# Last expert pair of a mixture-of-experts encoder layer: weights loaded in pieces, the waiting sums moved, the final norm shared among three engines

## What is computed

```python
def block_ffn(args):                  # one expert e and the tokens routed to it
    e, tok, wt = args
    xb = x_pad[tok]
    hid = jax.nn.silu(xb @ w1[e]) * (xb @ w3[e])     # 1024 -> 512, twice
    return (hid @ w2[e]) * wt[:, None]               # 512 -> 1024
...
x = x + g2 * moe_ffn(h, ...)
return rms_norm(x) * final_g          # x * rsqrt(mean(x*x) + eps) * final_g
```

## Time and profile before

| | |
|---|---|
| median of three runs | 721.17 us |
| the profiled execution | 720.32 us |
| its span, first to last instruction | 718.5 us |
| PE busy | 671.7 us (93%) |
| DVE, ACT, POOL busy | 346.4, 174.1, 56.0 us |
| read from memory | 252.84 MB |

### The profile page before, as it was taken

The page is one execution under the profiler, slowest core; times in us unless marked ns, Lnnn a source line. Parts: engine busy times, 40 slices in busy tenths (PEclk is TensorE's granted clock), DMA queues, the critical chain, the costliest instruction groups (busy, mean ns, idle before and its releaser), DMA issues.

```text
span 718.5 us, 9181 instructions
## 1 busy us (share of the span) xinstructions
PE 671.7 (93%) x3685; PEld 364.2 (51%) x3685; DVE 346.4 (48%) x648; ACT 174.1 (24%) x309; POOL 56.0 (8%) x55
## 2 busy tenths in 40 slices
PE   2799999999998799999999999898999999989893
PEld 2477787866878433443443443453434344334341
DVE  3554988798977713333333343333233443332236
ACT  4433468323324210210210210111021111110104
POOL 2016900100000100000000000000000000000000
PEclk9999999999999899999999999999999999999997
DMA  9998355665359699999999999999999999999952
GB/s 333 388 376 299 118 176 204 237 234 234 117 235 352 255 399 421 425 426 429 424 428 425 428 425 427 412 425 428 425 425 430 426 424 429 423 425 429 426 239 117
DMA packets 39147, 253.19 MB, mean 352 GB/s; under 512 B 4160, under 2 KB 4544, under 8 KB 26304
## 3 DMA queue, kind: packets, MB, share of 16 engines
q1 hardware_dynamic: 34560, 243.82, 83.1%
q0 software_dynamic: 2624, 4.74, 1.8%
q10 hardware_dynamic: 1920, 4.04, 1.5%
HBM read 252.84 MB, written 4.19 MB: 358 GB/s over the span
## 4 chain that ended last, share of the span: by engine, by line
PE 71%; DMA 21%; DVE 4%; SPq 1%; issue 1%; ACT 1%; POOLq 0%; DVEq 0%
PE bank L963 24%; PE bank L654 18%; DMA ring<-in_w 17%; PE bank L972 12%; DMA ring<-in_w_mod 3%; PE bank L980 3%; PE bank L981 2%; PE bank L926 2%; SPq L483 1%; PE bank L778 1%; DVE x L1825 1%; PE bank L1002 1%; DMA xg_rows<-x_rows,keep 1%; PE bank L934 1%; PE bank L606 1%
## 5 line engine op out<-in xcount | busy, mean ns | idle before, releaser
L963 PE MATMUL bank<-ring,low 128*64 128x512 f32 x944 | 228.2, 599 | 11.7 <-DMA ring<-in_w 11.0
L963 PEld LDWEIGHTS bank<-ring,low 128*64 128x64 f32 x944 | 75.0, 138 | 132.1 <-issue 131.0
L1825 DVE TENSOR_TENSOR x<-x,bank 128x512 f32<-128x512 f32 x136 | 84.4, 682 | 79.5 <-PE bank L981 79.5
L972 PE MATMUL bank<-ring,low 128*64 128x512 f32 x432 | 114.0, 596 | 1.0 <-DVE x L1825 0.9
L972 PEld LDWEIGHTS bank<-ring,low 128*64 128x64 f32 x432 | 35.0, 137 | 65.2 <-issue 63.5
L1815 DVE SCALAR_TENSOR_TENSOR y_raw<-bank,keep,g2b 128x512 f32<-128x512 f32 x32 | 24.0, 751 | 87.4 <-PE bank L972 87.4
L1936 DVE TENSOR_TENSOR low<-low,bank 128x512 f32<-128x512 f32 x16 | 11.0, 688 | 102.5 <-PE bank L963 102.5
L980 PE MATMUL bank<-y_hi,slot_tok 128*128 128x512 f32 x128 | 53.5, 418 | 0.2 <-DVE y_lo L1820 0.2
L981 PE MATMUL bank<-y_lo,slot_tok 128*128 128x512 f32 x128 | 50.3, 393 | 0.0
L1444 ACT COPY low<-bank 128x512 f32<-128x512 f32 x16 | 9.4, 586 | 165.0 <-PE bank L934 165.0
L1454 ACT CAST y_hi<-y_raw 128x512 fp32r<-128x512 f32 x32 | 19.8, 618 | 108.2 <-DVE y_raw L1815 108.2
(11 more groups left out here) (274 smaller groups left out, 880.6 us busy)
## 6 DMA issues: line engine op xcount, KB each, us to landing
ring<-in_w SPq DMA_DIRECT2D x82, 2048.0 KB, 26.6
ring<-in_w_mod SPq DMA_DIRECT2D x11, 2048.0 KB, 11.9
mid<-in_w SPq DMA_DIRECT2D x10, 2048.0 KB, 28.1
ring<-in_w_in SPq DMA_DIRECT2D x4, 2048.0 KB, 22.9
ring<-in_w SPq DMA_DIRECT2D x8, 1024.0 KB, 8.6
ring<-in_w_out SPq DMA_DIRECT2D x2, 2048.0 KB, 10.3
x<-in_x SPq DMA_DIRECT2D x4, 512.0 KB, 5.3
mid<-in_w_mod SPq DMA_DIRECT2D x1, 2048.0 KB, 23.8
```

Of the source, the lines that this page charges most:

```text
L963: last = mm(bk[e * CAP:(e + 1) * CAP, :], xb[:, k, e * CAP:(e + 1) * CAP], unit(n % SLOTS, KD)[:, k, :], start=k == 0, stop=k == KD - 1)
L972: last = mm(bk[e * CAP:(e + 1) * CAP, :], hid_t[:, k, e * CAP:(e + 1) * CAP], unit(n % SLOTS, KF)[:, k, hf * 512:(hf + 1) * 512], start=k ...
L1825: return v.tensor_tensor(acc[:, t, c], acc[:, t, c], bk[:, :], ALU.add)
```

## The change

- SP loads the last pair's units in pieces (`last_pair_units`). w1 and w3 come as two halves over k, the first halves of both experts ahead of the second halves. w2 comes as the left 512 columns, and the right 512 columns in two halves over k. A transfer for the first piece of the second expert now stands ahead of the second piece of the first. PE waits for the first pieces, and inside the products for the others.
- In the last pair the waiting sums use eight different banks and wait for no add. Of the second four, three are made after up product B and the fourth after `turn_hid`. The down product waits for four adds in place of eight.
- ACT loads the root's table after the last pair's hidden copy. DVE adds the first of the final sums between `weighted` and `low_part` of the second half.
- In the final norm ACT squares half rows: four left halves, one instruction that makes the root's bias of their sums, then for each tile the right half and the root. DVE scales the right halves alone. For the left halves GpSimd multiplies by final_g and ACT scales the product. A store waits for both.

```diff
+            def last_pair_units(k):
+                w, kk = ((w1_r, KD), (w3_r, KD), (w2_r, KF))[k // 2]
+                pieces = (((slice(0, kk // 2), slice(0, 512)), (slice(kk // 2, kk), slice(0, 512))) if k < 4 else
+                          ((slice(0, kk), slice(0, 512)), (slice(0, kk // 2), slice(512, D)),
+                           (slice(kk // 2, kk), slice(512, D))))
+                for i, (r, c) in enumerate(pieces):
+                    for e in range(2):
+                        n = FIRST[LAST] + k + e
+                        if i == 0:
+                            slot_used_up(n - SLOTS)
+                        src = w[:, bass.ds(experts_of(LAST)[e], 1), r, c].rearrange("p e k n -> p (e k) n")
+                        done = landed[n % SLOTS] if i == len(pieces) - 1 else (begun[k + e], middle_in[e])[i]
+                        sp.dma_start(unit(n % SLOTS, kk)[:, r, c], src).then_inc(done, 16)
...
-            for n in range(SLOTS + 4, UNITS):
+            for n in range(SLOTS + 4, FIRST[LAST]):
...
+            for k in range(0, UPP, 2):
+                last_pair_units(k)
...
             for t in range(NT):
                 sp.wait_ge(fin, t + 1)
+                sp.wait_ge(fin_low, t + 1)
...
+            def sum_bank(p, g):
+                return ((TB, CA, Y0, Y1, G0, G1, A1, A3) if p == LAST else SUM_BANKS + SUM_BANKS)[g]
...
+                        if k == KD // 2 and n0 == FIRST[LAST]:
+                            pe.wait_ge(landed[n % SLOTS], landed_at(n))
...
+                        if n0 == FIRST[LAST] and hf == 1:
+                            if k == 0:
+                                pe.wait_ge(middle_in[e], 16)
+                            elif k == KF // 2:
+                                pe.wait_ge(landed[n % SLOTS], landed_at(n))
...
-                    if g >= 4:
+                    if g >= 4 and p < LAST:
...
-                if before:
+                if p == LAST:
+                    pe.wait_ge(sil_ready, p + 1)
+                    combine_before(p, range(4, 7))
+                    summed(1)
+                elif before:
                     combine_before(p, range(4, 8))
-                summed(5)
+                    summed(5)
                 pe.wait_ge(hid_ready, p + 1)
                 turn_hid().then_inc(t_done, 1)
+                if p == LAST:
+                    combine_before(p, range(7, 8))
...
-                summed(8)
+                summed(4 if p == LAST else 8)
...
                 nc.scalar.copy(hid_t.rearrange("p k s -> p (k s)"), TB[:, :]).then_inc(hidt_ready, 1)
+                if to_come == 0:
+                    a(rstd[:, 0:1], col["eps"], ACT.Sqrt).then_inc(fin_table, 1)
...
+            def halfs_square(t, hf, sums):
+                act.wait_ge(acc_done, 8 * LAST + HALVES_FIRST.index(2 * t + hf) + 1)
...
+                a(unread, acc[:, t, c], ACT.Square, accum_out=sums[:, t:t + 1]).then_inc(fin_ssq, 1)
+
+            def low_half_scaled(t):
+                act.wait_ge(fin_rec, t + 1)
+                act.wait_ge(fin_gain, t + 1)
+                a(acc[:, t, 0:512], gained[:, t, :], ACT.Copy, scale=rstd[:, t:t + 1]).then_inc(fin_low, 1)
...
+            for t in range(NT):
+                halfs_square(t, 0, first_ssq)
+            act.wait_ge(fin_ssq, NT)
+            a(norm_bias, first_ssq, ACT.Identity, bias=col["eps"], scale=1.0 / D).then_inc(fin_bias, 1)
+            act.wait_ge(fin_bias, 1)
+            for t in range(NT):
+                halfs_square(t, 1, ssq)
+                act.wait_ge(fin_ssq, NT + t + 1)
+                a(rstd[:, t:t + 1], ssq[:, t:t + 1], ACT.Sqrt, bias=norm_bias[:, t:t + 1], scale=1.0 / D).then_inc(fin_std, 1)
+                if t > 0:
+                    low_half_scaled(t - 1)
+            low_half_scaled(NT - 1)
...
                     weighted(y_raw, p % BUFS, hf).then_inc(yf_ready, 1)
+                    if p == LAST and hf == 1:
+                        last_add(HALVES_FIRST[0])
...
-                v.scalar_tensor_tensor(acc[:, t, :], acc[:, t, :], rstd[:, t:t + 1], tail_fg,
+                v.scalar_tensor_tensor(acc[:, t, 512:D], acc[:, t, 512:D], rstd[:, t:t + 1], tail_fg[:, 512:D],
...
+            pool.wait_ge(tail_in, 16)
+            for t in range(NT):
+                pool.wait_ge(acc_done, 8 * LAST + HALVES_FIRST.index(2 * t) + 1)
+                g_.tensor_tensor(gained[:, t, :], acc[:, t, 0:512], tail_fg[:, 0:512], ALU.mult).then_inc(fin_gain, 1)
```

More of the change, by code:

```diff
@@ L67 @@
 HALVES_FIRST = (0, 2, 4, 6, 1, 3, 5, 7)
+LAST = PAIRS - 1
 AHEAD = 2
@@ L240, in build @@
         g2b = place("g2b", BIG + 3 * D, [P, D])
+        more_unread = place("more_unread", BIG + D, [P, 2, 512])
         onehot = place("onehot", LOW, [P, NT, P], BF16)
@@ L378, in build @@
         a_half = sem("first_pair_half_done")
+        begun = [sem(f"last_pair_begun{k}") for k in range(UPP)]
+        middle_in = [sem(f"last_pair_middle_in{e}") for e in range(2)]
         a_done, sil_ready, hid_ready, t_done, hidt_ready = sems(
@@ L386, in build @@
             "extra_transposed extra_hidt extra_down extra_yf extra_yh extra_yl extra_combined extra_added lists_chain")
-        fin_table, tail_in, fin_ssq, fin_std, fin_rec, fin, stored = sems(
-            "fin_table tail_in fin_ssq fin_std fin_rec fin stored")
+        fin_table, tail_in, fin_ssq, fin_std, fin_rec, fin, fin_low, fin_gain, fin_bias, stored = sems(
+            "fin_table tail_in fin_ssq fin_std fin_rec fin fin_low fin_gain fin_bias stored")
         block = ctx.enter_context(nc.Block())
@@ L419, in build @@
         tail_fg = ring[:, tail_slot, 0:D]
+        gained = ring[:, tail_slot, D:3 * D].rearrange("p (t n) -> p t n", t=NT)
+        first_ssq = ring[:, tail_slot, 3 * D:3 * D + NT]
+        norm_bias = ring[:, tail_slot, 3 * D + NT:3 * D + 2 * NT]
         w1_r = A["w1"][0].rearrange("e (p k) n -> p e k n", p=P)
@@ L562, in _ @@
                     further_rounds(sp, extra_units)
-            sp.wait_ge(y_done, 2 * (PAIRS - 1))
+            for k in range(0, UPP, 2):
+                last_pair_units(k)
+            sp.wait_ge(y_done, 2 * LAST)
             sp.dma_start(tail_fg, A["final_g"].rearrange("(a n) -> a n", a=1).to_broadcast([P, D])).then_inc(tail_in, 16)
@@ L1061, in combine_before @@
                 for g in groups:
-                    if g >= 4:
+                    if g >= 4 and p < LAST:
                         pe.wait_ge(acc_done, 8 * p - 8 + (g - 3))
-                    combine_group(g, (p - 1) % BUFS, y_hi, y_lo, SUM_BANKS[g % 4]).then_inc(c_done, 1)
+                    combine_group(g, (p - 1) % BUFS, y_hi, y_lo, sum_bank(p, g)).then_inc(c_done, 1)
             def combine_extra(p, t):
@@ L1084, in weights @@
                         n = n0 + 2 * k + e
-                        pe.wait_ge(landed[n % SLOTS], landed_at(n))
+                        if p == LAST:
+                            pe.wait_ge(begun[2 * k + e], 16)
+                        else:
+                            pe.wait_ge(landed[n % SLOTS], landed_at(n))
                 tile = 2 * (p - XPAIR - 1) if XPAIR < p <= LATER else None
@@ L1184, in _ @@
             pe.wait_ge(sil_ready, PAIRS)
+            pe.wait_ge(acc_done, 8 * LAST)
             for i, g in enumerate(HALVES_FIRST):
@@ L1482, in _ @@
                     further_rounds(act, another_block, extra_begin)
-            a(rstd[:, 0:1], col["eps"], ACT.Sqrt).then_inc(fin_table, 1)
             act.wait_ge(fin_table, 1)
-            for t in range(NT):
[L1487 to L1490, removed]
+            def halfs_square(t, hf, sums):
+                act.wait_ge(acc_done, 8 * LAST + HALVES_FIRST.index(2 * t + hf) + 1)
+                c = slice(hf * 512, (hf + 1) * 512)
+                unread = xg_rows[:, t * 512:(t + 1) * 512] if t < 2 else more_unread[:, t - 2, :]
+                a(unread, acc[:, t, c], ACT.Square, accum_out=sums[:, t:t + 1]).then_inc(fin_ssq, 1)
[3 more added lines that the diff above has]
+                a(acc[:, t, 0:512], gained[:, t, :], ACT.Copy, scale=rstd[:, t:t + 1]).then_inc(fin_low, 1)
+            for t in range(NT):
+                halfs_square(t, 0, first_ssq)
[9 more added lines that the diff above has]
+            low_half_scaled(NT - 1)
         @block.vector
@@ L1825, in add_group, with last_add @@
                 return v.tensor_tensor(acc[:, t, c], acc[:, t, c], bk[:, :], ALU.add)
+            def last_add(g):
+                i = HALVES_FIRST.index(g)
+                dve.wait_ge(c_done, 8 * LAST + i + 1)
+                add_group(g, EXTRA_BANKS[i]).then_inc(acc_done, 1)
             def add_up(p, groups):
@@ L1829, in add_up @@
                     dve.wait_ge(c_done, 8 * p - 8 + (g + 1))
-                    add_group(g, SUM_BANKS[g % 4]).then_inc(acc_done, 1)
+                    add_group(g, sum_bank(p, g)).then_inc(acc_done, 1)
             dve.wait_ge(job_done, len(JOBS))
@@ L1983, in _ @@
                     further_rounds(dve, another_block, extra_begin)
```

(5 more changed lines are left out.)

## The result

The changed kernel takes 717.79 us (median of seven runs, 716.41 to 718.63) against 721.51 for the kernel before (seven runs, 719.72 to 722.65): a ratio on record of 0.9942, with a 95% interval of 0.9927 to 0.9957, so a gain of 3.1 to 5.3 us. The profiled execution took 716.96 us, with a span of 715.1.

What follows compares the result with a forecast made beforehand. The expert weights bound the kernel, so only work after the last weights could shrink. From the runs' median, 721.17 - 3.65 (PE in the last pair), with 0 for everything else, gave 717.5 us; range 715.6 to 720.1.

Steps and rivals of the forecast that it cites:

- Step 1: PE in the last pair: earlier up products, moved sums and earlier down product gain 2.30 + 0.82 + 0.49 + 0.04 = 3.65 us.
- Step 2: Last pair's weight stream: fourteen transfers replace six, about 2 us more issuing, all hidden, 1.4 us left in hand.
- Step 3: DVE's final adds: one moves ahead of the last `low_part`; the last ends 6.2 us after the last `weighted` starts.
- Step 4: Final norm on ACT: last scaling 12.1 us after `weighted` starts, against 12.5; stores return the 0.4, so 0.
- Step 5: GpSimd's products beside DVE's last `low_part`: no cost, 0; at worst 0.9 us.
- the first rival: GpSimd holds DVE: the final adds wait for its products, 3.5 us come back, 721.0, no change; chance 0.14.
- the upper bound of the tail: End after the last `weighted` starts: +0.9 us, from non-overlapping roots and bias (five times 0.1) and the store's 0.4.
- the second: Rival: each transfer has its own price in the queue, 1.45 us; time 727.8, slower; chance 0.07.
- the third: Rival: the pieces don't help, as first halves land hardly ahead; 2.30 us stays lost, 719.8, no change; chance 0.05.

Runs made afterwards that it cites:

- whole_again: Second run of the changed kernel with the last pair's six units loaded whole again, as before the change: 719.34 us (1 run).
- old_sums: Changed kernel with the last pair's waiting sums back in four banks and the down product behind all eight adds: 718.28 us, ratio 0.9955 to the kernel before.
- pieces_alone: Kernel before with only the last pair's pieces and PE's waits for them; banks, sums, norm and GpSimd as before: 718.08 us, ratio 0.9953 to the kernel before.
- old_norm: Changed kernel with the whole-tile final norm of ACT and DVE back, GpSimd idle, moved add kept: 716.68 us, ratio 0.9940 to the kernel before.
- pool_early: Changed kernel with one more GpSimd product, read by nothing, released by the last weighted step: 717.71 us (1 run).
- quarters: Changed kernel with the last w1 and w3 in quarters over their rows in place of halves: 717.66 us, ratio 0.9950 to the kernel before.
- whole_units: Changed kernel with the last pair's six units loaded whole again, as before the change: 721.09 us, ratio 0.9990 to the kernel before.

## Why the prediction was right

The forecast was 717.5 us and the median is 717.79. Against the runs of before, 721.51 - 717.79 = 3.72 us were gained where 3.65 were forecast. That they lie so close is in part luck: in the traces S and the tail give 3.9, of which the tail's 0.4 was not forecast and 0.15 of step 1 did not come. The mechanism of the gain, PE's two waits for whole units, is the one that was forecast. By step:

- **Step 1** (PE, -3.65) measured -3.50. The mechanism holds piece by piece: `whole_again` gives 2.96 for the pieces (2.30 + 0.82 in the forecast), `old_sums` 0.63 for the sums (0.49 + 0.04). Each is worth 0.1 more beside the other: alone the pieces give 2.86 (`pieces_alone`) and the sums 29.96 - 29.42 = 0.54. Term by term, between the lines of the earlier trace rows and those after, the four gains are 2.13, 0.76, 0.45 and 0.15 us, where 2.30, 0.82, 0.49 and 0.04 were forecast. PE's new waits cost nothing: products with a wait inside take 7.07 and 7.09, as before. The mis-sized term is the step from one product to the next, which was put at 0.22 us and is 0.39 (673.45 to 673.84). The 0.22 is an average; PE's records come in couples 0.03 us apart, with 0.4 us to the next couple, as three lines from the kernel before show, too:

```profile
672.46 0.59 PE L972 MATMUL bank<-ring,low 128*64 128x512 f32 x1
672.49 0.59 PE L972 MATMUL bank<-mid,low 128*64 128x512 f32 x1
672.89 0.59 PE L972 MATMUL bank<-ring,low 128*64 128x512 f32 x1
```

- **Step 2** (pieces hidden) is right in its result and wrong in one term: "SP issues each in about 0.35 us". The pieces took up to 8.9. The stream did not run dry, because 32 us of loading were queued, as the step had said, and PE waited for none of them: the tightest, the second half of w3, landed at 686.05, 0.4 us before up B came to it (0.5 forecast), and the last of w2 at 696.5, 1.6 us ahead. The rate fell as forecast: 382 GB/s in 685 to 690 us, beside the 387 of the earlier trace rows, and w2 took 10.4 us where 10.8 were taken. The late final_g cost nothing, as GpSimd needs it only after D.
- **Step 3** (the add, last at D + 6.2) measured D + 6.3. The add is worth 0.61 at the end with the norm as before (it was not taken away under the shared norm); the prediction's sum has no term of its own for it, as step 4 let ACT's work set the end.
- **Step 4** (tail 0, after a gain of 0.4 given back) measured -0.43. The left-half scaling came each 0.61 us, not 0.76, so the last one ended at D + 11.4, not 12.1. The stores took back 0.65 to 0.75 (from the last scaling to the end it is 3.8 us, against 3.1 before and 3.04 in `old_norm`), not 0.5. The account is therefore 0.61 from the add, and a loss of 0.27 from sharing the norm; the 0.09 that is left is within the reading of the spans.
- **Step 5** (GpSimd, 0) held, by 0.06 us, in every trace with this order. `pool_early` shows what the other order costs: 0.64, inside the bound of 0.9.

Three readings of the prediction are off, and nothing hung on them: the earlier trace rows goes from 399 to 430 GB/s, not 434; the first rival's 721.0 lies 0.9 us beyond the range, not two; and the upper bound of the tail seems to count the store's 0.4 a second time.

Of the rivals, the first falls by the adds' 0.61 us, the second by `quarters`, the third by `whole_units` and `pieces_alone`. What the third feared is there, and large: the sixteen parts of one piece land over some 10 us (676.3 to 686.05 for the last of w3). But the slow parts lag alike, as the prediction had argued: the four pieces of w1 are complete at 668.6, 671.1, 673.6 and 676.1. `old_norm` has the lowest median (716.68), but its interval and the changed kernel's cover each other; only its tail, 0.27 shorter, says that GpSimd and ACT's share in the norm could be dropped.

## What to carry to other kernels

When a stream of loads ends last, the work behind the final transfer counts, not the load: cut the last units so that the consumer begins on the first half and has only a quarter product to do after the last byte. Once the chain of waits holds no transfer any more, as here, finer pieces bring nothing (`quarters`). Before sharing a last stage among engines, ask what its stores do: results that are ready closer together than one store takes wait in the queue. A share that looks free on an idle engine can still block another engine, and which of the two starts first decides it.

## What the runs showed of the hardware that was not expected

- Pieces that are queued behind much other loading can hold the queue that issues them: 8.9 us in one instruction for 512 runs of 2 KB, up to 4.2 for 128 runs of 8 KB, against 0.33 to 0.38 for the last whole units before the change. Everything behind them on that queue moves too (final_g by 13 us).
- In a queue that does not run empty, cutting the loads finer costs little: 0.06 to 0.09 us for each added transfer.
- The sixteen parts of one transfer of the last weights landed over some 10 us.
- After an idle time of about 2 us the tensor engine's clock was granted at half for some 4 us in one execution, and stayed full in two others with the same idle time (the kernel before and `whole_again`).
- A DVE product of two SBUF inputs went from 0.69 to 1.30 us when a GpSimd product had begun 0.5 us ahead of it, and lost nothing when it was itself 0.06 us ahead.
